# Norms by token halves, and the first feed-forward step in full precision, in a two-block network on one core

## The reference

```python
def rmsnorm(x, g):
    xf = x.astype(jnp.float32)
    y = xf * lax.rsqrt(jnp.mean(xf * xf, axis=-1, keepdims=True) + EPS)
    return (y * g.astype(jnp.float32)).astype(x.dtype)

# first block, layer l (mix and ffn norms have a gain only)
h = rmsnorm(x, norm_mix)
...                                   # projections, four branches, gates, lifts
x = x + merged @ w_out
hf = rmsnorm(x, norm_ffn)
gate, up = jnp.split(hf @ ffn_w_up, 2, axis=-1)
x = x + (silu(gate) * up) @ ffn_w_down

# second block, layer i (the modulation is a product of a conditioning vector)
sh1, sc1, g1, sh2, sc2, g2 = jnp.split(silu_c @ mod_w[i] + mod_b[i], 6, axis=-1)
a = rmsnorm_2(h, norm1_w[i]) * (1 + sc1) + sh1
ac = rmsnorm_2(hc, norm1_w[i]) * (1 + csc1) + csh1     # context tokens, layer 0 only
m = ab_mixer(a, ac, ...) if i == 0 else hyena_mixer(a, ...)
h = h + g1 * m
h = h + g2 * swiglu(rmsnorm_2(h, norm2_w[i]) * (1 + sc2) + sh2, w1, w3, w2)
...
return rmsnorm_2(h, final_norm_w)
```

## Time and profile before

| | |
|---|---|
| median of three runs | 2558.67 us (2557.29 to 2560.15) |
| the profiled execution | 2562.15 us, its span 2560.4 us |
| mean granted TensorE clock | 0.934 |
| PE, DVE, ACT, POOL busy | 2306.1, 1236.7, 743.9, 56.9 us |
| instructions | 32758 |

### The profile page before, as it was taken

How to read it: one execution, slowest core, us unless ns; L and a number is a source line. 1 busy time by engine, 2 the same in 40 slices (tenths; PEclk the granted TensorE clock), 3 DMA queues, 4 the chain that set the end, 5 groups by cost and what they waited for, 6 DMA issues and landing times.

```text
span 2560.4 us, 32758 instructions
## 1 busy us (share of the span) xinstructions
PE 2306.1 (90%) x13870; PEld 1906.8 (74%) x13870; DVE 1236.7 (48%) x1990; ACT 743.9 (29%) x950; POOL 56.9 (2%) x78
## 2 busy tenths in 40 slices
PE   6999989899989998998998899897789979988996
PEld 5867768589978577785997776884469966645996
DVE  3331338588623314344886332667445534543543
ACT  3113430234311325203333332122334421003442
POOL 0000000000000000000000000000010000000000
PEclk9999989999989989899999899988689989999998
DMA  6333336577643324265786012000155523202551
GB/s 215 133 115 115 118 113 214 182 263 263 212 118 135 115 83 148 85 229 197 263 280 216 4 66 99 2 2 34 33 176 190 187 99 107 99 0 95 189 186 66
DMA packets 206647, 348.57 MB, mean 136 GB/s; under 512 B 19555, under 2 KB 110442, under 8 KB 206117
## 3 DMA queue, kind: packets, MB, share of 16 engines
q1 hardware_dynamic: 191632, 291.09, 33.7%
q0 software_dynamic: 14592, 55.31, 6.4%
q10 hardware_dynamic: 276, 0.08, 0.0%
HBM read 345.41 MB, written 1.05 MB: 135 GB/s over the span
## 4 chain that ended last, share of the span: by engine, by line
PE 75%; DVE 15%; ACT 6%; issue 3%; DMA 0%; SPq 0%; DVEq 0%; ACTq 0%
PE psum L366 50%; PE psum L689 21%; DVE ring_low L977 3%; DVE A L1368 3%; DVE G L1060 2%; PE psum L426 1%; ACT high_weights L970 1%; DVE wide_room L1060 1%; ACT A L746 1%; ACT xn L753 1%; PE psum L410 1%; ACT L760 1%; DVE tmp L1060 1%; DVE x L1060 1%; DVE xn L1030 1%
## 5 line engine op out<-in xcount | busy, mean ns | idle before, releaser
L366 PE MATMUL psum<-hT,ring 128*128 128x256 f32 (+1 forms) x2784 | 622.7, 385 | 1.4 <-ACT hT L776 1.4
L366 PEld LDWEIGHTS psum<-hT,ring 128*128 128x128 f32 (+1 forms) x2784 | 531.3, 192 | 81.5 <-issue 5.6
L977 DVE TENSOR_TENSOR ring_low<-ring,high_weights 128x2048 fp32r<-128x2048 f32 x132 | 302.6, 2292 | 227.0 <-ACT high_weights L970 225.0
L689 PE MATMUL psum<-high_rows,high_weights 128*128 128x256 f32 x1408 | 399.4, 284 | 12.7 <-DVE ring_low L977 10.1
L689 PE MATMUL psum<-high_rows,ring_low 128*128 128x256 f32 x1408 | 395.4, 281 | 0.0
L689 PE MATMUL psum<-hT_low,high_weights 128*128 128x256 f32 x1408 | 395.4, 281 | 0.0
L689 PEld LDWEIGHTS psum<-high_rows,high_weights 128*128 128x128 f32 x1408 | 266.8, 189 | 17.1 <-issue 13.2
L689 PEld LDWEIGHTS psum<-hT_low,high_weights 128*128 128x128 f32 x1408 | 266.7, 189 | 0.6
L970 ACT ACTIVATE high_weights<-ring 128x2048 fp32r<-128x2048 f32 x132 | 253.1, 1917 | 45.7 <-DMA ring<-in_ffn_w_up_dram 41.7
L689 PEld LDWEIGHTS psum<-high_rows,ring_low 128*128 128x128 f32 x1408 | 266.3, 189 | 0.0
L1368 DVE SCALAR_TENSOR_TENSOR A<-A,silu_c 128x256 f32<-128x256 f32 x392 | 190.1, 485 | 14.0
(11 more groups left out here) (414 smaller groups left out, 2524.7 us busy)
## 6 DMA issues: line engine op xcount, KB each, us to landing
ring<-in_w_in_dram SPq DMA_DIRECT2D x36, 2048.0 KB, 7.8
ring<-in_ffn_w_dram SPq DMA_DIRECT2D x66, 1024.0 KB, 5.3
A<-in_mod_w_dram POOLq DMA_DIRECT2D x48, 1024.0 KB, 7.8
ring<-in_ffn_w_up_dram SPq DMA_DIRECT2D x44, 1024.0 KB, 5.5
ring<-in_ffn_w_down_dram SPq DMA_DIRECT2D x22, 1024.0 KB, 5.9
ring<-in_w_lift_dram SPq DMA_DIRECT2D x16, 1024.0 KB, 8.7
ring<-in_ab_w_in_dram SPq DMA_DIRECT2D x7, 2048.0 KB, 8.0
ring<-in_hy_w_in_dram SPq DMA_DIRECT2D x6, 2048.0 KB, 7.9
```

Source lines behind the costliest of these rows:

```text
L366: return pe.eng.matmul(out, lhsT, rhs, start=(k == 0), stop=(k == n - 1))
L689: ins = pe.eng.matmul(out, lhs[a], rhs[b], start=first and n == 0, stop=last and n == 2)
L977: v.eng.tensor_tensor(low, whole, high.bitcast(F32), ALU.subtract).then_inc(*v.mark(f"w_lo/{l}.{i}"))
```

## The change

- A norm goes by token halves. ACT squares one half (`squared`), VectorE makes the reciprocal root by an integer first guess and three Newton steps (`stats`, 9 dependent ops on one column; no ln, no exp), scales that half's rows (`norm_rows`), TensorE transposes it in two banks (`norm_turned`), and the copies follow (`norm_out`: one op for each bank on VectorE where there is a gain only; with a shift, four ops on VectorE for one bank and four on ACT for the other). The first half's transposes stand ahead of the last k of the last `out` or mixer output group, and the second half's in the middle of the next product.
- The products behind a norm go by halves too: a_x, the first `hy_in` panel (`transposed_by_half`), and step 0 of each FFN. Step 0 multiplies plain fp32 rows and weights (`raw_hT`), without high and low parts; the rows' low part (`norm_low`) has a buffer of its own and is made for step 1.
- `down` 9 moves into the last step: half 0 takes `down` 9 and 10, then half 1; each half is marked by itself (`ffn_half`), and residual, squares and rows follow by halves.
- The norm of ctx moves into the FFN of layer 1: rows at j = 6, transposes at j = 8 and 9; the DMA of ctx moves in POOL's queue ahead of the loads of mod_w 33. lv is the first panel of the second block; its ctx tokens come before x's. `gate2`'s rows are spread after step 0 of FFN 2 and 3. Three of the five gains are made in FFN 1.
- The roots for q, mq, o, gq and the heads are 11 dependent ops on VectorE (`root`) instead of ACT's ln and exp with a Newton step.
- mem's transposes come after a_b. x is loaded, and the output stored, in two DMAs of 0.5 MB.

```diff
+        def norm_turned(key, t):
+
+            rows = rows_of.get(key, xn)
+            pe.wait_ge(*reached(f"xn/{key}.{t}"))
+            for g in range(2):
+                label = f"xnT_ready/{key}.{t}.{g}"
+                b = fixed(label, 4 + 2 * t + g) if key == "mem" else take(label)
+                for i in range(4):
+                    k = 4 * g + i
+                    ins = pe.eng.transpose(b[:, i * P:(i + 1) * P], rows[:, t, k * P:(k + 1) * P], ident[:, :])
                 ins.then_inc(*pe.mark(label))
 
...
+        def transposed_by_half(names, labels, key, w, used, read=None):
+
+            b = [take(label) for label in labels]
+            for t, tok in enumerate(TOKENS):
+                for u in range(2):
+                    for c in range(2):
+                        if (t, u, c) == (0, 1, 1):
+                            norm_turned(key, 1)
+                        for k in range(KD):
+                            if u == 0 and c == 0 and k % 4 == 0:
+                                pe.wait_ge(*reached(f"hT/{key}.{t}.{k // 4}"))
+                            ins = mm(b[u][:, c * SEQ + t * P:c * SEQ + (t + 1) * P],
+                                     w[:, k, (2 * u + c) * P:(2 * u + c + 1) * P], hT[:, k, tok], k, KD)
+                    if t:
+                        ins.then_inc(*pe.mark(labels[u], [used] if u else []))
+
...
+                        if (half, t, k) == (1, 1, KD - 1):
+                            norm_turned(f"ffn{l}", 0)
                         ins = mm(b, top["mergedT"][:, k, t * P:(t + 1) * P], w[:, k, :], k, KD)
...
+                if j == 0:
+                    labels = [f"{('ffn_gate', 'ffn_up')[g]}_ready/{l}.0" for g in range(2)]
+                    b = [banks.take(label) for label in labels]
+                    for t, tok in enumerate(TOKENS):
+                        for g in range(2):
+                            w, used = panel(f"up{l}.0.{g}")
+                            for c in range(2):
+                                if (t, g, c) == (0, 1, 1):
+                                    top["pe_norm"](key, 1)
+                                for k in range(KD):
+                                    if g == 0 and c == 0 and k % 4 == 0:
+                                        pe.wait_ge(*reached(f"raw_hT/{key}.{t}.{k // 4}"))
+                                    ins = mm(b[g][:, c * SEQ + t * P:c * SEQ + (t + 1) * P], w[:, k, c * P:(c + 1) * P],
+                                             hT[:, k, tok], k, KD)
+                            if t:
+                                ins.then_inc(*pe.mark(labels[g], [used]))
+                    if l in top["gate_spread"]:
+                        top["gate_spread"][l]["pe"]()
+                elif j < FFN_STEPS:
                     for g in range(2):
                         w, used = panel(f"up{l}.{j}.{g}")
                         label = f"{('ffn_gate', 'ffn_up')[g]}_ready/{l}.{j}"
                         b = banks.take(label)
                         wh, wl = parts(PIECES.index((False, j, g)))
                         for c in range(2):
-                            for k in range(KD):
-                                if j == 0 and g == 0 and c == 0 and k % 2 == 0:
-                                    pe.wait_ge(*reached(f"{need}.{k // 2}"))
-                                cols = slice(c * P, (c + 1) * P)
-                                ins = product(b[:, c * SEQ:(c + 1) * SEQ], (wh[:, k, cols], wl[:, k, cols]),
-                                              (hT_high[:, k, :], top["hT_low"][:, k, :]), k == 0, k == KD - 1)
+                            ins = up_product(b, c, wh, wl, f"hT/{key}" if (j, g, c) == (1, 0, 0) else None)
                         ins.then_inc(*pe.mark(label, [used]))
-                if j > 0:
+                if 0 < j < FFN_STEPS - 1:
                     i = j - 1
                     if i == 0:
                         acc = banks.fixed(f"ffn_ready/{l}", 4, 4)
-                    w, used = panel(f"down{l}.{i}")
-                    wh, wl = parts(PIECES.index((True, i, 0)))
-                    pe.wait_ge(*reached(f"act_lo/{l}.{i}"))
+                    wh, wl, used = down_parts(i)
                     for t in range(MT):
-                        for half in range(2):
-                            for c in range(2):
-                                tok, cols = slice(t * P, (t + 1) * P), slice(half * HALF, (half + 1) * HALF)
-                                ins = product(acc[:, 2 * t + half, :],
-                                              (act_high[:, i % 2, c, tok], top["act_low"][:, i % 2, c, tok]),
-                                              (wh[:, c, cols], wl[:, c, cols]), i == 0 and c == 0,
-                                              i == FFN_STEPS - 1 and c == 1)
-                    ins.then_inc(*pe.mark(f"down_done/{l}.{i}", [used] + ([f"ffn_ready/{l}"] if i == FFN_STEPS - 1 else [])))
+                        ins = down_product(i, t, wh, wl)
+                    ins.then_inc(*pe.mark(f"down_done/{l}.{i}", [used]))
+                if j == FFN_STEPS:
+                    for t in range(MT):
+                        for i in (FFN_STEPS - 2, FFN_STEPS - 1):
+                            wh, wl, used = down_parts(i)
+                            ins = down_product(i, t, wh, wl)
+                            if t:
+                                ins.then_inc(*pe.mark(f"down_done/{l}.{i}", [used] + ([f"ffn_ready/{l}", f"ffn_half/{l}.1"] if i == FFN_STEPS - 1 else [])))
+                            elif i == FFN_STEPS - 1:
+                                ins.then_inc(*pe.mark(f"ffn_half/{l}.0"))
...
+        def stats(key, t):
+
+            s, half, y, tmp = (st[:, i + t:i + t + 1] for i in (0, 2, 4, 6))
+            v.wait_ge(*reached(f"sumsq/{key}.{t}"))
+            e.tensor_scalar(half, s, -0.5 / D, -0.5 * EPS, ALU.mult, ALU.add).then_inc(*v.mark(f"ms/{key}.{t}"))
+            v.wait_ge(*v.own())
+            e.tensor_scalar(y.bitcast(I32), half.bitcast(I32), 1, None, ALU.logical_shift_right).then_inc(*v.mark())
+            v.wait_ge(*v.own())
+            e.tensor_scalar(y.bitcast(I32), y.bitcast(I32), -1.0, float(0x5F3759DF + 0x40000000 - 0x400000), ALU.mult,
+                            ALU.add).then_inc(*v.mark())
+            v.wait_ge(*v.own())
+            for i in range(3):
+                e.tensor_scalar(tmp, y, y, half, ALU.mult, ALU.mult).then_inc(*v.mark())
+                v.wait_ge(*v.own())
+                e.scalar_tensor_tensor(y, tmp, 1.5, y, ALU.add, ALU.mult).then_inc(*v.mark())
+                v.wait_ge(*v.own())
+
+        def norm_rows(key, t, src):
+
+            stats(key, t)
+            e.tensor_scalar(rows_of.get(key, xn)[:, t, :], src[:, t, :], st[:, 4 + t:5 + t], None, ALU.mult).then_inc(*v.mark(f"xn/{key}.{t}"))
+            v.wait_ge(*v.own())
+
...
+        def root(y, ms, tmp, scale=1.0):
+
+            bits = y.bitcast(I32)
+            e.tensor_scalar(bits, ms.bitcast(I32), 1, None, ALU.arith_shift_right).then_inc(*v.mark())
             v.wait_ge(*v.own())
+            e.tensor_scalar(bits, bits, -1.0, float(0x5F3759DF), ALU.mult, ALU.add).then_inc(*v.mark())
+            v.wait_ge(*v.own())
+            for by in (1.0, 1.0, scale):
+                e.scalar_tensor_tensor(tmp, y, -0.5 * by, y, ALU.mult, ALU.mult).then_inc(*v.mark())
                 v.wait_ge(*v.own())
+                e.tensor_tensor(tmp, tmp, ms, ALU.mult).then_inc(*v.mark())
+                v.wait_ge(*v.own())
+                e.scalar_tensor_tensor(y, tmp, 1.5 * by, y, ALU.add, ALU.mult).then_inc(*v.mark())
+                v.wait_ge(*v.own())
+
...
+        def ffn_residual(l, t):
+
+            v.wait_ge(*reached(f"ffn_half/{l}.{t}"))
+            b = B(f"ffn_ready/{l}")
+            for half in range(2):
+                r = x[:, t, half * HALF:(half + 1) * HALF]
+                tt(r, r, b[:, 2 * t + half, :], ALU.add, f"x/{l}.{2 * t + half}", [f"read ffn_ready/{l}"] if t and half else ())
+
...
+            if l == 1 and j == 0:
+                top["gains"](range(3))
+            if l == 1 and j == CTX_SCALED:
+                for t in range(MT):
+                    top["dve"]["norm_rows"]("ctx", t, top["ctx_rows"])
+            if l == 1 and j in CTX_TURNS:
+                top["dve"]["norm_out"]("ctx", CTX_TURNS.index(j), top["gain"][:, 0, :], top["mod"][:, 0, 0:8, 1])
...
+    plan = ["lv", "gk", "gv", "gq", "small2", "lqk", "lg", "gz", "ab_out.0", "ab_out.1"]
...
+        w, used = panel("lv")
+        tokens("lv", w, [], 0, lambda t: hTs[0])
+        tokens("lv", w, [used], 1, lambda t: hTs[1][2 * t:2 * t + 2])
         w, used = panel("gk")
-        transposed("gk", w, [], 0, need=hTs[0])
-        transposed("gk", w, [used], 1, need=hTs[1])
+        transposed("gk", w, [], 0)
+        transposed("gk", w, [used], 1)
...
+            ffn_add(3, t)
+            stats("final", t)
+            v.wait_ge(*reached("final_row/0"))
...
```

(7 more changed lines are left out.)

439 lines of the change are left out of this document (247 added, 192 removed).

## The result

The changed kernel takes 2495.69 us (median of four runs, 2489.41 to 2500.92) against 2559.41 for the kernel before (four runs): ratio 0.9749, 95% interval 0.9724 to 0.9774. 2479 was predicted, a gain of 80; 63.7 came, so the time lies in the stated range but above the 2470 to 2490 that had 72 in 100.

The account below looks back on a forecast made before the run. TensorE's stream was taken as the bound, with a hole it waits for at each of nine norms. Gains summed to 80.0 us, 2558.67 to 2479; range 2458 to 2512, with 2470 to 2490 given 72 in 100.

Parts of the forecast that it names:

- X: Reference time in the prediction: the end of TensorE's last group before an FFN.
- Rival A: In projections and FFN steps by halves, half records cost up to a whole record's 0.230 us: +99, 2578 us; 4 in 100.
- Rival C: The holes at the norms close better than the working, by half of 26 us: 2466 us; 10 in 100.
- rival B: Second half comes late behind half 0's copy on VectorE; 4.2 us unhidden at seven places, 29 lost: 2508 us; 14 in 100.
- the entries of FFN 0 and 1: From X into the first two FFNs: up(1) at X + 18.4, 10.9 to 11.0 us gained each, 22.0 together.
- Half 1's 64 records end at E + 35.0: FFN 2 to the hyena input: the projection ends there instead of at E + 46.7, gaining 11.7 us.
- E: Reference time in the prediction: the end of an FFN's last `up` product.
- Up(1) at X + 22.2: Entries of FFN 2 and 3: up(1) there instead of X + 28.7 and X + 28.1, gaining 6.5 and 5.8 us.
- gk's first 14 records ... 0.9 more. 25.4: FFN 1 to the second block: lv first covers x's norm, gk's records cost 0.230 not 0.286; 25.4 us gained.
- Start: 1.1: Kernel start to a_x: one half's squares and the root instead of table loads gain 1.1 us, between 0 and 4.
- Output, 4.6: After the last FFN: half 1 leaves at 14.6, end at E + 26.7 instead of E + 31.3, gaining 4.6 us.
- -1.9: FFN 1: ctx's 16 transposes add 1.9 us; its rows, 5.1 of VectorE, fall in step 6's slack.

Follow-up runs that it names:

- u2: Changed kernel with step 0 of the FFNs in fp32 over all 256 tokens at once, second half's transposes ahead of it; span 2519.0 us (+25.1).
- u3: Changed kernel with lv back behind lk and x's transposes ahead of gk, ctx's norm still inside FFN 1; span 2508.1 us (+14.2).
- e6: e5 with the output's adds of both halves ahead of either root, and the rows' low part at x1tok's place; 2475.2 us, ratio 0.9668 to the kernel before.
- e1: Changed kernel with down 9 multiplied for both halves, then down 10 for both; 2488.39 us, ratio 0.9722 to the kernel before.
- e3: Changed kernel with gate 2's row moved from behind step 0 to behind step 1's products in FFN 2 and 3; one run, 2494.1 us.
- e7: e6 without the buffer's move, TensorE taking step 0's second bank only ahead of its first product; 2475.48 us, ratio 0.9667 to the kernel before.
- b1: Kernel before, with only the rows' low part of FFN 2 and 3 in its own buffer; act(1) to act(10) takes 1.8 and 1.9 us more.
- experiment 6: Comparison of executions where no edit acts: act(10) of FFN 0 to act(0) of FFN 1 is 514.0 us in b1, 519.9 in the kernel before.
- e8: e7 with SyncE issuing the 1 MB load of mem behind the first weight panel instead of ahead; 2475.28 us, ratio 0.9668 to the kernel before.
- e5: Changed kernel with the edits of e1, e3 and e4 together; 2479.52 us, ratio 0.9685 to the kernel before.
- e4: Changed kernel with VectorE taking the last modulation sum of FFN 0 and 1 behind half 0's rows, not ahead of its adds; one run, 2488.64 us.
- u1: Changed kernel with step 0 of the four FFNs back to three fp32r products over all 256 tokens; span 2525.1 us (+31.2).

## Why the prediction was right, and where its sum was off

The time lay in the range, and the mechanism was as said: the holes close, the half records cost half a record, lv covers x's norm (some 20 for the overlap at the entries by u2, 13.7 for lv's order by u3, 3.5 for the two roots of the heads in the trace). The price of a record was read from rows that held some low clock and a last record's end: 0.230 and 0.119, where the pace at a clock of 1.00 is 0.216 and 0.112. The second made up(1) come 17.2 behind X in FFN 0 and 1 and not 18.4. Rival A, half records at the price of whole ones, is excluded by 0.111 a record. Rival C failed. Of rival B one place of seven came true: the output, where half 1 stood behind half 0's chain (e6).

But for the entries of FFN 0 and 1 (0.6 more than said) every term of the sum came out too large, by 19 us together; 4.8 us that are no gain of the change (below) make up for a part of that, and this is luck. The steps that were mis-sized:

- "Half 1's 64 records end at E + 35.0" (FFN 2 to the hyena input, 11.7). They ended at E + 38.1: in the wait for `down` 10's low part the clock fell, and half 0's transposes started at E + 18.5 and not 15.9. Transposes and copy then took 2.7 and not 1.7, and the 48 half records behind them 7.2 and not 5.7, which covered the wait for half 1 (1.3 predicted). The working had 5.95 for the end of the wait and no price for the clock behind this wait and the next. e1 removes the first wait: the transposes start 2.5 earlier, but half 1 ends only 0.8 earlier, at E + 37.3, as TensorE then waits 2.9 longer for half 0's rows and the clock falls there. So what ends last there in e1 is VectorE's chain to the rows.
- "Up(1) at X + 22.2" in FFN 3 (5.8, measured 2.1). The bank wait of 2.1 us was foreseen in the start at X + 3.4, but behind it the clock fell, 48 half records took 7.22 and not 5.6, and the gate's row waited 2.0 more where 0.4 was allowed: its second bank was read by act(0), which stands behind two low parts on VectorE. Behind this second wait of 1.7 the clock fell again, and the 96 records of up(1) took 12.81 and not 11.66. (28.1 less 22.2 is 5.9, the sum has 5.8.) In FFN 2 the same bank wait left the clock up (5.60), and only the row's wait was missed. e3 shows the row's wait, e7 the bank's. The windows of the 48 records in FFN 3 and in FFN 2:

```profile
2279.70:2286.70 7.00, 7.00 (x48) 7.00 (x49) 2.51 (x10) 1.09 (x2) 0.00 (x0) 0.76 0.77 283
1826.40:1831.70 5.30, 5.30 (x48) 5.30 (x49) 2.51 (x10) 1.08 (x2) 4.84 (x9) 1.00 1.08 391
```

- The steps of FFN 2 and 3, costed at nothing, took 3.7 more. The rows' low part in a buffer of its own has a price of 1.8 and 1.9 for the two (b1), which is all of it. That it is the place of this buffer is shown; what about the place makes it is open, since another place (e6) has the slow pace as well.
- "gk's first 14 records ... 0.9 more. 25.4": the stretch with the heads gave 25.7 of 29.0. lv itself ended at E + 44.1 as said (E + 44.4). 2.9 of the difference are the small products behind the transposes, which take 8.7 us at a granted clock of 0.61 where they took 5.8 at 1.00 before. u3 shows that it isn't lv's place. Nor is it the change: b1, the kernel before but for one buffer, has 8.6, and the other executions have 7.2 or 8.7. So the 5.8 was how the kernel before happened to run, as in experiment 6.
- "Start: 1.1": -1.7. VectorE's copies of half 0 started at 23.3 us and would have let the products start at 24.1 (e8), but the panel of a_x came at 24.97. The working has what the norm saves and not what is late next: a DMA, and behind it the low clock. The products start 2.0 earlier than before, but the first 26 of them come every 0.213 us, 2.6 more than at a clock of 1.00. e8 gets 0.8 of the wait back and 1.0 of the clock.
- Output, 4.6 against 4.0: the adds of half 1 start at E + 16.6, behind half 0's scaling, and not at 14.6; the store took 3.1 where 4.5 was taken.
- "**-1.9**" for ctx's 16 transposes: the steps of FFN 0 and 1 took 2.9 more. 2.3 of them came in FFN 1, which has the work for ctx, and 0.6 in FFN 0, which hasn't; no run separates them.

On the other side 4.8 us came in mixer 1, where nothing was changed that is on the path. b1 has them too: that is how the kernel before happened to run when it was profiled, and no gain of the change.

The best version here is e5 with the output's adds first (e6): 2475.2 us, ratio 0.9668 to the kernel before and 20 us below the changed kernel; e7 and e8 are equal to it within the intervals.

## What to carry to other kernels

When a unit of work is split into halves to overlap, walk through each in-order engine with both halves: the second half's first instruction can stand behind the last of the first half's chain (the output), and the order (piece, half) or (half, piece) decides whether a part that is made late is waited for. The start is the same case: half 0's copies stand behind half 1's root and rows. Price a wait on TensorE with what may follow it: the waits of 2.1 to 3.3 us here cost their own length, or up to twice that when the clock fell. And when a wait is removed, ask which wait ends last then: at FFN 2 the next one took up two thirds of the gain. And a single profiled execution holds chance of some 5 us in a stretch: compare stretches that the edit doesn't touch first.

## What was not expected of the hardware

- A half record of 128 columns in a long stream takes 0.111 to 0.112 us, and the 72-column records of the earlier trace rows come every 0.112 as well (the 0.115 there holds the end of the last one), while 256-column ones come every 0.216, all at a granted clock of 1.00. So below 128 columns a narrower fp32 record saved nothing; what sets that floor no run here shows. The 16 transposes of the earlier trace rows come every 0.109, and the 0.119 holds the end of the last one.
- The clock's fall is not bound to a wait's length. Waits of 2.85 (FFN 0) and 3.29 us (FFN 2) brought it to 0.50 in the changed kernel, waits of the same length ahead of the same products (FFN 1, output) did not. Nor is it bound to the place: at FFN 0 the same wait slowed the products in four of six executions (changed kernel, e3, u2, u3) and not in e4 and u1, at FFN 1 in two, at FFN 2 in five, at the output in two. A wait of 2.1 us did it in FFN 3 and not in FFN 2, in all seven executions that have it (changed kernel, e1, e3, e4, e5, e6, u3).
- In FFN 2 and 3 the same up products come every 0.117 us with the rows' low part on top of hT and every 0.119 with it in either of two other places, at a granted clock of 1.00 in all.
